# Expert weights of a mixture of experts: ten places with a 2 MB load each become five pairs of places with a 4 MB load each

## The reference

```
def expert_step(acc, p):
    w1, b1, w2, b2, ce = p            # w1 (1024, 2048), w2 (1024, 1024)
    u = t @ w1 + b1
    g = jnp.minimum(u[:, :D_FF], SWIGLU_LIMIT)
    lin = jnp.clip(u[:, D_FF:], -SWIGLU_LIMIT, SWIGLU_LIMIT)
    a = g * jax.nn.sigmoid(SWIGLU_ALPHA * g) * (lin + 1)
    y = a @ w2 + b2
    return acc + ce[:, None].astype(y.dtype) * y, None
```

## Time and profile before

| | us |
|---|---|
| median of three runs | 1367.12 |
| the profiled execution | 1366.06 |
| its span | 1364.3 |
| TensorE busy | 1317.0 |
| VectorE busy | 473.9 |
| ScalarE busy | 327.5 |

### The profile page before, as it was taken

The page is one execution under the profiler, slowest core; times in us unless marked ns, Lnnn a source line. Parts: engine busy times, 40 slices in busy tenths (PEclk is TensorE's granted clock), DMA queues, the critical chain, the costliest instruction groups (busy, mean ns, idle before and its releaser), DMA issues.

```text
span 1364.3 us, 16054 instructions
## 1 busy us (share of the span) xinstructions
PE 1317.0 (97%) x6489; PEld 679.6 (50%) x6489; DVE 473.9 (35%) x802; ACT 327.5 (24%) x476; POOL 21.4 (2%) x39
## 2 busy tenths in 40 slices
PE   7999999999999999999999999999999999999995
PEld 7889997988888333333333333333333333333331
DVE  4754545444656322322223222322223222322223
ACT  5564545464444100110011000100011001110002
POOL 2000000000101000000000000000000000000000
PEclk9999999999999999999999999999999999999998
DMA  9354443545568999999999999999999999999993
GB/s 315 138 198 160 139 170 124 211 160 211 185 244 331 407 427 430 432 431 430 431 432 431 431 431 431 433 431 430 431 432 430 431 431 431 434 430 431 432 430 160
DMA packets 68233, 475.06 MB, mean 348 GB/s; under 512 B 8480, under 2 KB 10592, under 8 KB 43616
## 3 DMA queue, kind: packets, MB, share of 16 engines
q1 hardware_dynamic: 66048, 473.01, 83.7%
q10 hardware_dynamic: 2144, 1.47, 0.4%
HBM read 473.42 MB, written 1.05 MB: 348 GB/s over the span
## 4 chain that ended last, share of the span: by engine, by line
PE 81%; DMA 13%; ACT 2%; DVE 1%; SPq 1%; issue 1%; ACTq 0%; DVEq 0%
PE bank L1472 44%; PE bank L1297 17%; DMA place<-in_w_exp_in 12%; PE bank L1286 7%; PE bank L1557 4%; PE bank L1485 1%; ACT fxqT L808 1%; PE bank L1529 1%; PE bank L1501 1%; DMA fxv<-in_mem 1%; PE bank L1521 1%; PE bank L1473 1%; PE bank L1410 1%; PE bank L1429 1%; DVE w_lo L870 1%
## 5 line engine op out<-in xcount | busy, mean ns | idle before, releaser
L1472 PE MATMUL bank<-place,fxqT 128*64 128x512 f32 x1536 | 688.0, 597 | 22.1 <-ACT fxqT L808 15.6
L1473 PE MATMUL bank<-place,fxqT 128*64 128x512 f32 x1536 | 688.1, 597 | 0.0
L1472 PEld LDWEIGHTS bank<-place,fxqT 128*64 128x64 f32 x1536 | 199.2, 137 | 422.1 <-issue 389.6
L1148 DVE TENSOR_SCALAR big_a<-bank 128x512 f32<-128x512 f32 x32 | 22.1, 692 | 525.2 <-PE bank L1473 525.2
L870 DVE TENSOR_TENSOR w_lo<-ring,w_hi 128x2048 fp32r<-128x2048 f32 x64 | 146.7, 2291 | 153.5 <-ACT w_hi L571 153.3
L1473 PEld LDWEIGHTS bank<-place,fxqT 128*64 128x64 f32 x1536 | 199.2, 137 | 0.0
L571 ACT ACTIVATE w_hi<-ring 128x2048 fp32r<-128x2048 f32 x64 | 122.7, 1918 | 158.7 <-PE bank L1297 113.9
L805 ACT ACTIVATE big_a<-big_a 128x512 f32<-128x512 f32 x32 | 20.1, 630 | 435.3 <-DVE big_a L1148 435.3
L1176 DVE TENSOR_TENSOR xs<-bank,xs 128x512 f32<-128x512 f32 x132 | 81.9, 683 | 24.3 <-PE bank L1557 24.3
L1297 PE MATMUL bank<-w_hi,h_hi 128*128 128x512 f32 x224 | 88.3, 394 | 0.1
L1297 PE MATMUL bank<-w_hi,h_lo 128*128 128x512 f32 x224 | 87.3, 390 | 0.0
(11 more groups left out here) (269 smaller groups left out, 1272.6 us busy)
## 6 DMA issues: line engine op xcount, KB each, us to landing
place<-in_w_exp_in SPq DMA_DIRECT2D x128, 2048.0 KB, 28.2
place<-in_w_exp_out SPq DMA_DIRECT2D x64, 2048.0 KB, 28.5
ring<-in_w_in SPq DMA_DIRECT2D x19, 2048.0 KB, 7.6
ring<-in_w_branch SPq DMA_DIRECT2D x6, 2048.0 KB, 7.6
ring<-in_w_mem_kv SPq DMA_DIRECT2D x4, 2048.0 KB, 7.7
ring<-in_w_out SPq DMA_DIRECT2D x2, 2048.0 KB, 12.4
ring<-in_w_in SPq DMA_DIRECT2D x2, 1024.0 KB, 7.5
xs<-in_x SPq DMA_DIRECT2D x2, 512.0 KB, 4.3
```

The lines of the kernel that those rows point to most:

```text
L1148: dve.tensor_scalar(gate.rearrange("c (q p) -> c q p", q=4), bank[0][:, :].rearrange("c (p q) -> c q p", q=4), LIMIT, None, ALU.min).then_ ...
L1472: mm(o[0:CAP, :], lhsT, low, start=start, stop=stop)
L1473: return mm(o[CAP:P, :], lhsT, high, start=start, stop=stop)
```

## The change

The ten places are now the halves of five `pair` tensors. The fill is the same: the same ten 2 MB loads, in the same order, at the same points; each raises its pair's `pair_in` by 16, so that a filled pair stands at 32. Behind the fill `load_pair` issues one 4 MB load for a pair, when the whole pair is used. For `w_exp_in` this load has one run of 32 KB per partition; for `w_exp_out` two runs of 16 KB per partition, 2 MB apart in memory. TensorE waits once per pair, before its first piece, and raises `pair_used` once, behind its second piece.

```diff
-        place = [sb(f"place{b}", [P, KT // 2, 2 * UW]) for b in range(PLACES)]
+        pair = [sb(f"pair{d}", [P, 2, KT // 2, 2 * UW]) for d in range(PAIRS)]
+        place = [pair[b // 2][:, b % 2, :, :] for b in range(PLACES)]
...
-            def load_piece(r, m, c):
-
-                b, used = piece_turn(r, m, c)
-                sp.wait_ge(place_used[b], used)
-                load(m * TURN + c // PIECES, c % PIECES, b)
+            def load_pair(r, m, c):
+
+                d, used = pair_turn(r, m, c)
+                e = m * TURN + c // EXPERT_PAIRS
+                at = slice(e, e + 1) if isinstance(e, int) else bass.ds(e, 1)
+                part = c % EXPERT_PAIRS
+                sp.wait_ge(pair_used[d], used)
+                if part < W1 // 2:
+                    src = w_exp_in[0, at][:, D // 2 * part:D // 2 * (part + 1), :].rearrange("e (p q) n -> p (e q n)", q=4)
+                    sp.dma_start(pair[d][:, :, :, :].rearrange("p b k n -> p (b k n)"), src).then_inc(pair_in[d], 16)
+                else:
+                    src = w_exp_out[0, at].rearrange("e (b p q) n -> p (e b) (q n)", b=2, q=4)
+                    sp.dma_start(pair[d][:, :, :, :].rearrange("p b k n -> p b (k n)"), src).then_inc(pair_in[d], 16)
...
@@ TensorE, layer one
-                    b, used = piece_turn(r, m, PIECES * q + j)
-                    pe.wait_ge(place_in[b], used * 16 + 16)
-                    rows_ = place[b][:, :, :].rearrange("p (q a) n -> p q (a n)", q=2)
+                    d, used = pair_turn(r, m, EXPERT_PAIRS * q + half)
+                    if j % 2 == 0:
+                        pe.wait_ge(pair_in[d], used * 16 + 32)
+                    rows_ = pair[d][:, j % 2, :, :].rearrange("p (q a) n -> p q (a n)", q=2)
...
-                    ins.then_inc(place_used[b], 1)
+                    if j % 2 == 1:
+                        ins.then_inc(pair_used[d], 1)
...
@@ TensorE, layer two
-                    b, used = piece_turn(r, m, PIECES * q + W1 + j)
-                    pe.wait_ge(place_in[b], used * 16 + 16)
+                    d, used = pair_turn(r, m, EXPERT_PAIRS * q + W1 // 2)
+                    if j == 0:
+                        pe.wait_ge(pair_in[d], used * 16 + 32)
...
-                    ins.then_inc(place_used[b], 1)
+                    if j == W2 - 1:
+                        ins.then_inc(pair_used[d], 1)
```

More of the change, by code:

```diff
@@ L30 @@
 PLACES = 10
+PAIRS = PLACES // 2
+EXPERT_PAIRS = PIECES // 2
 TURN = 5
@@ L110, with pair_uses @@
 }
-def place_uses(b):
-    return -(-(NE * PIECES - b) // PLACES)
+def pair_uses(d):
+    return -(-(NE * EXPERT_PAIRS - d) // PAIRS)
 def turn(bank, user):
@@ L279, in build @@
         weights_rounded, weights_split = sem("weights_rounded"), sem("weights_split")
-        place_in = [sem(f"place_in{b}") for b in range(PLACES)]
-        place_used = [sem(f"place_used{b}") for b in range(PLACES)]
+        pair_in = [sem(f"pair_in{d}") for d in range(PAIRS)]
+        pair_used = [sem(f"pair_used{d}") for d in range(PAIRS)]
         o_rounded, o_split = sem("o_rounded"), sem("o_split")
@@ L346, in slot_weights, with pair_turn @@
             return r[:, KT // 2 * half:KT // 2 * (half + 1), :], hi, lo
-        def piece_turn(r, m, c):
-            b = c % PLACES
-            return b, r * place_uses(b) + m * CYCLE + c // PLACES
+        def pair_turn(r, m, c):
+            d = c % PAIRS
+            return d, r * pair_uses(d) + m * CYCLE + c // PAIRS
         def for_experts(eng, r, expert):
@@ L389, in load @@
                     src = w_exp_out[0, at][:, FF // 2 * half:FF // 2 * (half + 1), :].rearrange("e (p q) n -> p (e q n)", q=4)
-                sp.dma_start(place[b][:, :, :].rearrange("p k n -> p (k n)"), src).then_inc(place_in[b], 16)
+                sp.dma_start(place[b].rearrange("p k n -> p (k n)"), src).then_inc(pair_in[b // 2], 16)
             for u, (name, kind, j) in enumerate(UNITS):
@@ L434, in _ @@
                 load(1, j, PIECES + j)
-            def load_piece(r, m, c):
-                b, used = piece_turn(r, m, c)
-                sp.wait_ge(place_used[b], used)
-                load(m * TURN + c // PIECES, c % PIECES, b)
+            def load_pair(r, m, c):
[10 more added lines that the diff above has]
+                    sp.dma_start(pair[d][:, :, :, :].rearrange("p b k n -> p b (k n)"), src).then_inc(pair_in[d], 16)
             with sp.Fori(0, NE // TURN) as m:
[L443 to L446, removed]
+                for c in range(PAIRS, PAIRS + TURN * EXPERT_PAIRS):
+                    load_pair(0, m, c)
+            for c in range(PAIRS, NE % TURN * EXPERT_PAIRS):
+                load_pair(0, NE // TURN, c)
             sp.wait_ge(route_ready, 1)
@@ L452, in _ @@
                         with sp.Fori(0, NE // TURN) as m:
[L453 to L456, removed]
+                            for c in range(TURN * EXPERT_PAIRS):
+                                load_pair(r, m, c)
+                        for c in range(NE % TURN * EXPERT_PAIRS):
+                            load_pair(r, NE // TURN, c)
             for t in range(TT):
@@ L812, in expert @@
                                ACT.Copy).then_inc(selWT_ready, 1)
-                b, used = piece_turn(r, m, PIECES * q + PIECES - 1)
-                act.wait_ge(place_used[b], used + 1)
+                d, used = pair_turn(r, m, EXPERT_PAIRS * q + EXPERT_PAIRS - 1)
+                act.wait_ge(pair_used[d], used + 1)
                 act.activation(yS, bank[5][:, :], ACT.Copy).then_inc(yS_ready, 1)
@@ L1149, in expert @@
                                   LIMIT, None, ALU.min).then_inc(gate_ready, 1)
-                b, used = piece_turn(r, m, PIECES * q + W1 - 1)
-                dve.wait_ge(place_used[b], used + 1)
+                d, used = pair_turn(r, m, EXPERT_PAIRS * q + W1 // 2 - 1)
+                dve.wait_ge(pair_used[d], used + 1)
                 dve.tensor_scalar(lin.rearrange("c (q p) -> c q p", q=4), bank[1][:, :].rearrange("c (p q) -> c q p", q=4),
@@ L1538, in expert @@
                 for j in range(W2):
-                    b, used = piece_turn(r, m, PIECES * q + W1 + j)
-                    pe.wait_ge(place_in[b], used * 16 + 16)
+                    d, used = pair_turn(r, m, EXPERT_PAIRS * q + W1 // 2)
+                    if j == 0:
+                        pe.wait_ge(pair_in[d], used * 16 + 32)
                     for k in range(4):
-                        w = place[b][:, k, :]
+                        w = pair[d][:, j, k, :]
                         ins = both_halves(bank[5], aT[:, k, j, :], w[:, 0:512], w[:, 512:D], False,
                                           j == W2 - 1 and k == 3)
-                    ins.then_inc(place_used[b], 1)
+                    if j == W2 - 1:
+                        ins.then_inc(pair_used[d], 1)
                     if j == 0:
```

## The result

The change makes the kernel slower by about 5 us: 1372.5 us (median of seven runs, 1371.25 to 1374.17) against 1367.5, a ratio of 1.0039 with an interval of 1.0027 to 1.0051. The prediction was 1371.1 us, between 1369.0 and 1375.0.

The account below looks back on a forecast made before the run. The prediction took the stream of weight transfers to bound the kernel, ending with expert 31's piece 3 plus TensorE's work behind it. Start +3.39, end +3.43 and rate -2.8 gave +4.0 us: 1371.1 us, range 1369.0 to 1375.0.

Parts of the forecast that it names:

- Who sets the end: Expert stage: the stream of transfers sets the end, 1.3 us an expert slower than TensorE, up to expert 31's piece 3.
- the waits begin six experts earlier and not three: Sign in the expert stage: TensorE's waits for pairs begin some three experts earlier, each ahead of piece 2.
- The start, +3.39: Behind the fill: SyncE's first load goes out at 456.01 instead of 452.62 us, into an empty stream, 3.39 us later.
- I take nothing for this: Third pair's release, 476.20 us: the stream does not run dry again; cost 0, with 0.5 us kept in the range.
- The end, +3.43: Last expert, layer one: TensorE still has piece 2 to do after the last wait, 3.43 us more.
- The cover of layer two's wait: Last expert: layer two's pair lands 9.73 us later, TensorE asks after 11.99 us, so the wait is covered by 2.3.
- The rate, -2.8: Stream behind the fill: 32 KB runs need fewer packets; 570 saved per engine at 4.9 ns, 2.8 us less.
- the first rival: Runs are still cut to 16 KB, only small packets saved, 0.4 us: +6.4 us, 1373.5 us; chance 0.13.
- The second: Rival: each transfer has a fixed cost, at least 15 ns over 90 pairs; no change, 1369.2 us; chance 0.12.
- The 4.9 ns: DMA stream: cost of any packet beside its bytes, from 2 KB and 16 KB runs; rounding bounds given as 4.0 to 5.8.
- The slower pattern, the last rival: Layer two's pairs, runs 2 MB apart, move at 408 GB/s: +17 us together, 1388 us; chance 0.10.
- The sum: Whole kernel: +3.39 + 3.43 - 2.8 = +4.0 us, giving 1371.1 us.

Follow-up runs that it names:

- c_runs16: The change, but layer one's 4 MB load has two runs of 16 KB per partition instead of one of 32 KB: 1374.25 us, +7.2 against the kernel before.

## Why the prediction was right, and where it was not

**Who sets the end.** Right: TensorE's work is the same and the kernel is slower. With only the release changed it loses 4.8 us that TensorE's lead does not hide. That the waits begin six experts earlier and not three fits the two costs together: 4.3 + 3.4 us at 1.3 us an expert; three is what one of them would give.

**The start, +3.39.** Right in kind and size: 1.30 MB or 3.0 us are missing after 12 us.

**"I take nothing for this".** This step failed. The prediction let the pairs ahead end at 477.3 us, 1.1 us behind the third pair's load, and kept 0.5 us for it. Two things were wrong. The pairs ahead ended sooner: 0.4 us behind the load. And the load did not move bytes when it was issued: nearly 1 us passed until its first packets, a time that the prediction did not count, though the trace of before holds it (first load at 452.62 us, its first packets at 453.6). So the stream stood for half a us and took until 479 us to fill again. 4.3 us were missing after 90 us, where the start alone explains 3.0 to 3.4, so this term is +0.9 to +1.3. The run with three pairs by pieces moved the stop to the next release and halved the loss; the run with ten, where the lead had grown, lost nothing in the stream.

**The end, +3.43.** Right: 8.80 - 5.37 = 3.43 us in the chain, and 3.5 us between the two runs that differ in it. The cover of layer two's wait was right for the change; what was not said is that it ends when this term does.

**The rate, -2.8.** Right: 58.17 in place of 58.36 us for two experts are 0.10 us an expert, 2.9 us over thirty, and runs of 16 KB in the same transfers fall 2.0 to 2.4 us behind, where 2.4 were reckoned. 32 KB count as one packet in the profile (59096 packets in all, 68233 before), so the first rival is out. The second is out by c_runs16: with 4 MB transfers and 16 KB runs the rate rises by 0.3 GB/s, where a fixed 15 ns a transfer would have made it 0.9. The 4.9 ns held: in the nine traces with 32 KB runs the stream moves 432.3 to 432.8 GB/s between 600 and 1100 us, and 4.9 ns give 432.7. The Trainium skill's three cycles ("DMA: Bandwidth & Descriptors", "Why small descriptors are slow (HBM only)"), 3.5 ns by the prediction's estimate, give 432.3, the lower edge of these traces. The bounds that the prediction put on its 4.9 ns were misworked: half a unit of the 2.04 MB moves it by 0.2 ns, to 4.7 or 5.1, not to 4.0 or 5.8. The slower pattern, the last rival, does not occur: a stretch that holds both kinds of pair moves at 432.8 GB/s, and in c_runs16, where every pair has two runs 2 MB apart, the rate is 431.6, no lower than the 431.3 of before.

**The sum.** With the measured terms it is 4.3 + 3.4 - 2.9 = 4.8 us, against 5.0 and 5.9 in two sets of runs. The predicted +4.0 is 1.0 short of the first, about the term that was left out; the range was wide enough for it. In the profiled pair the difference of the spans is larger, 6.8 us: 0.6 are from before the experts, and the last wait came 1.3 us later than the missing bytes say (3.0 against 1.7), of which the odd 58.70 us of the last two experts are 0.5. Why a piece lands later than the bytes moved so far would say, and by different amounts in different executions, stays open, and with it why the gain of the long packets does not show fully when both ends are mended.

## What to carry to other kernels

In a ring of buffers whose transfers set the pace, coarser units cost something in two places. One is the first release behind the fill: the stream runs dry until the larger unit is used up. The other lies behind the last wait, where one more piece of work is left. A long steady middle costs nothing and gains a few nanoseconds a packet. Mending one tight release can move the stop to the next tight one, and taking work from behind the last wait uncovers the wait after it, so both have to be followed until the lead has grown. In judging whether a load comes in time, count from its first packets and not from its issue: here nearly 1 us lay between. And where the work outruns the transfers by only 1.3 us an expert, a wait that costs 3.43 us cannot be won back in the last expert alone.

## What the runs showed of the hardware

One run of 32 KB per partition counts as one packet, and 4.9 ns a packet beside its bytes, worked out from runs of 2 and 16 KB, give the change's 500 us in the middle (9605 packets, 216.39 MB) within 0.03%; the other traces with 32 KB runs are within 0.1%. From a load's issue to its first packets nearly 1 us passed where the stream had run out or was about to (452.62 to 453.6 us before, 456.68 to 457.7 and 476.82 to 477.75 in the change). A stream that had run dry took about 3 us to be full again (213, 262 and 328 GB/s in the first three). The last transfer drained over 2 to 3 us, by different amounts in two executions; that the 16 DMA engines end a transfer apart from one another is argued from this and not shown.
